# Moving four quads of V gathers per tile from the attention heads to the output and query projections, with the copy of the finished sums behind them

## The reference, cut to what matters

```python
q = (xb @ w_query).reshape(T, PEER_HEADS, 2, PEER_HALF)
s = jnp.einsum('thcd,hcnd->thcn', q, sub_keys)
sa, ia = lax.top_k(s[:, :, 0], PEER_TOPK)
...
top_s, top_j = lax.top_k(cand, PEER_TOPK)
eidx = jnp.take_along_axis(cidx, top_j, axis=-1)
gate = jax.nn.softmax(top_s.astype(jnp.float32), axis=-1).astype(xb.dtype)
act = jax.nn.gelu(jnp.einsum('thkd,td->thk', expert_u[eidx], xb), approximate=False)
return jnp.einsum('thk,thkd->td', gate * act, expert_v[eidx])
```

## Time and profile before

| what | value |
|---|---|
| median of 3 runs | 2177.47 us (2175.39 to 2177.49) |
| the profiled execution's own time | 2178.01 us |
| its span, first to last instruction | 2175.9 us |
| PE busy | 1216.6 us, 56% of the span |
| DVE busy | 1261.5 us, 58% |
| POOL busy | 1174.1 us, 54% |
| ACT busy | 374.3 us, 17% |
| moved by DMA | 722.04 MB, mean 332 GB/s |
| software DMA queue (the gathers) | 624.01 MB |

### The profile page before, as it was taken

How to read it: one execution, slowest core, us unless ns; L and a number is a source line. 1 busy time by engine, 2 the same in 40 slices (tenths; PEclk the granted TensorE clock), 3 DMA queues, 4 the chain that set the end, 5 groups by cost and what they waited for, 6 DMA issues and landing times.

```text
span 2175.9 us, 15704 instructions
## 1 busy us (share of the span) xinstructions
PE 1216.6 (56%) x4932; PEld 541.1 (25%) x4932; DVE 1261.5 (58%) x2795; ACT 374.3 (17%) x1034; POOL 1174.1 (54%) x1197
## 2 busy tenths in 40 slices
PE   5898778474885335853455574445667322223454
PEld 2544343233331233411222231122332000000110
DVE  3344430876485997776664678667477665555001
ACT  1221211011031011211121121112113100001211
POOL 3012110241457763577767457776745767777773
PEclk9798889785898557866567796666778656555887
DMA  9211274484899998999999999999999999999997
GB/s 338 94 59 39 77 275 133 164 302 162 343 372 379 410 380 321 371 361 410 409 389 403 410 384 371 410 409 395 408 411 349 375 409 409 409 409 409 411 409 295
DMA packets 204306, 722.04 MB, mean 332 GB/s; under 512 B 23248, under 2 KB 25536, under 8 KB 203072
## 3 DMA queue, kind: packets, MB, share of 16 engines
q0 software_dynamic: 171168, 624.01, 73.7%
q1 hardware_dynamic: 33056, 97.03, 12.1%
HBM read 704.71 MB, written 15.70 MB: 331 GB/s over the span
## 4 chain that ended last, share of the span: by engine, by line
PE 25%; DMA 24%; DVE 16%; POOL 14%; issue 5%; ACT 4%; DVEq 0%; POOLq 0%; ACTq 0%
DMA arena<-peer_expert_v,idx_v 16%; POOL arena L595 10%; DVE arena L1384 7%; PE PD L1041 6%; DMA arena<-peer_expert_u,idx_all 5%; POOL arena L589 4%; PE PB L1251 4%; PE PD L963 3%; PE PB L1230 3%; PE PA L1230 2%; DMA lev<-w_out 2%; PE PA L1181 2%; DMA lev<-peer_w_query 2%; DVE w L1521 1%; DVE lev L1501 1%
## 5 line engine op out<-in xcount | busy, mean ns | idle before, releaser
L589 POOL DMA_INDIRECT arena<-peer_expert_u,idx_all x576 | 545.5, 947 | 462.5 <-DVE arena L1384 218.7
L1384 DVE SCALAR_TENSOR_TENSOR arena<-arena,PC 128x1024 f32<-128x1024 f32 x576 | 675.5, 1217 | 149.7 <-DMA arena<-peer_expert_u,idx_all 143.8
L595 POOL DMA_INDIRECT arena<-peer_expert_v,idx_v x576 | 571.8, 993 | 252.0 <-issue 145.4
L1041 PE MATMUL PD<-arena,diag_v 128*32 128x512 f32 x1792 | 362.4, 887 | 516.5 <-DMA arena<-peer_expert_v,idx_v 490.7
L1041 PEld LDWEIGHTS PD<-arena,diag_v 128*32 128x32 f32 x1792 | 79.9, 141 | 758.8 <-issue 758.8
L817 ACT ACTIVATE diag_v<-consts,gate_all 128x32 f32<-128x32 f32 x576 | 138.1, 310 | 585.7 <-PE PD L1041 462.2
L963 PE MATMUL PD<-arena 128*128 128x512 f32 x384 | 175.8, 613 | 0.0
L1041 PE MATMUL PA<-arena,diag_v 128*32 128x512 f32 x512 | 87.0, 813 | 78.2 <-DMA arena<-peer_expert_v,idx_v 78.2
L1230 PE MATMUL PB<-lev,rows_t 128*128 128x512 f32 x160 | 86.6, 700 | 18.1 <-DMA lev<-w_out 12.4
L963 PEld LDWEIGHTS PD<-arena 128*128 128x128 f32 x384 | 74.0, 197 | 86.4 <-issue 85.9
L1449 DVE TENSOR_TENSOR PA<-PA,consts 128x128 f32<-128x128 f32 (+4 forms) x56 | 14.0, 250 | 139.1 <-PE PA L1099 138.8
(11 more groups left out here) (271 smaller groups left out, 1509.9 us busy)
## 6 DMA issues: line engine op xcount, KB each, us to landing
lev<-w_out SPq DMA_DIRECT2D x40, 512.0 KB, 9.2
lev<-peer_w_query SPq DMA_DIRECT2D x40, 512.0 KB, 7.8
arena<-w_in SPq DMA_DIRECT2D x8, 2048.0 KB, 14.2
arena<-peer_expert_u,idx_all POOLq DMA_INDIRECT x576, 9.7
arena<-peer_expert_v,idx_v POOLq DMA_INDIRECT x576, 10.2
arena<-w_in POOLq DMA_DIRECT2D x4, 2048.0 KB, 8.5
act<-staged SPq DMA_DIRECT2D x4, 1796.0 KB, 7.2
staged<-arena POOLq DMA_DIRECT2D x5, 1024.0 KB, 5.6
```

Source lines behind the costliest of these rows:

```text
L589: pool.indirect_dma_start(slot, None, peer_expert_u[0], bass.IndirectOffsetOnAxis(ap=idx_all[:, k:k + 1], axis=0)).then_inc(arrived, 16)
L595: pool.indirect_dma_start(slot, None, peer_expert_v[0], bass.IndirectOffsetOnAxis(ap=idx_v[:, k:k + 1], axis=0)).then_inc(arrived, 16)
L1041: ins = pe.matmul(psum[c * STRIP:(c + 1) * STRIP, half * 512:(half + 1) * 512], diag_v[:, at * STRIP:(at + 1) * STRIP], ring[slot_of[v_pla ...
L1384: eng.scalar_tensor_tensor(out=slot, in0=slot, scalar=1.0, in1=h2_dots[:, :], op0=ALU.mult, op1=ALU.mult, accum_out=out).then_inc(free, 1)
```

## The change

In tiles 3 and 4, four quads are taken from `head1`, `head3`, `head5` and `head7`. Two of them are placed at `rows`, between the output projection and the transposes of the normed rows, and two at `pq0`, between the halves of the query projection. The number of quads left over from `top` is 19 before and after. ACT's copy of the finished sums, which stood after `gram2`, now stands after `pq1`, behind the evacuation of the second query half. SP's store of them follows the last weight loads. ACT writes the diagonals of `pq0` ahead of its wait for the first query half. The copy and the store move in tiles 2, 3 and 4.

```diff
-LEFT_PLACES = [("start", 1)] + [(f"head{h}", 1) for h in range(HEADS)] + [
-    ("levels", 3), ("masks", 3), ("gram1", 2), ("gram2", 2)]
+LEFT_PLACES = [("start", 1)] + [(f"head{h}", 1) for h in range(0, HEADS, 2)] + [
+    ("levels", 3), ("masks", 3), ("gram1", 2), ("gram2", 2), ("rows", 2), ("pq0", 2)]
...
-            for place in [place for place, _ in DOT_PLACES + NEXT_PLACES] + ["end", "last", "rest"]:
+            for place in [place for place, _ in DOT_PLACES + [("pq0", 0)] + NEXT_PLACES] + ["end", "last", "rest"]:
...
-                if t > 1:
-
-                    sp.wait_ge(y_part_ready, t - 1)
-                    sp.dma_start(y_dram[t - 2], h2[:, :]).then_inc(y_part_saved, 16)
                 sp.wait_ge(x1_ready, t + 1)
                 sp.dma_start(x1_dram[t], xm).then_inc(x1_saved, 16)
...
                 for c in range(DC + WO_RING, 2 * DC):
                     sp.wait_ge(wo_used, 2 * DC * t + c - WO_RING + 1)
                     load_w_out(c)
+                if t > 1:
+
+                    sp.wait_ge(y_part_ready, t - 1)
+                    sp.dma_start(y_dram[t - 2], h2[:, :]).then_inc(y_part_saved, 16)
...
-                if t > 1:
-
-                    eng.wait_ge(v_free, values_before(t - 1))
-                    if t > 2:
-                        eng.wait_ge(y_part_saved, 16 * (t - 2))
-                    eng.activation(h2[:, :], PD[:, :], ACT.Copy).then_inc(y_part_ready, 1)
                 eng.wait_ge(ho_done, HG * (t + 1))
...
+                diagonals(t, "pq0")
                 eng.wait_ge(pq_done, t + 1)
                 nq = P if t else N_SAMPLE
                 eng.activation(w1[0:nq, 0:D], PB[0:nq, :], ACT.Copy).then_inc(pq_evac, 1)
-                diagonals(t, "pq0")
                 eng.wait_ge(wo_used, 2 * DC * (t + 1))
                 eng.activation(w1[0:nq, D:2 * D], PA[0:nq, :], ACT.Copy).then_inc(pq_evac, 1)
                 diagonals(t, "pq1")
+                if t > 1:
+
+                    eng.wait_ge(v_free, values_before(t - 1))
+                    if t > 2:
+                        eng.wait_ge(y_part_saved, 16 * (t - 2))
+                    eng.activation(h2[:, :], PD[:, :], ACT.Copy).then_inc(y_part_ready, 1)
```

## The result

The change makes the kernel slower: 2204.4 us median (2204.14 to 2206.64, 4 runs) against 2177.48 us (2175.39 to 2179.11, 4 runs). The ratio is 1.0124, 95% interval 1.0111 to 1.0138. That is 26.9 us more, where 2226 us was forecast with a range from 2206 to 2249. The direction was right and the place was right.

What follows compares the result with a forecast made beforehand. Gathers and loads at the memory limit (409 to 412 GB/s) bound heads and query stage. Per tile 36.2 + 4.4 + 0.8 = 41.4 us lost, 18 given back, 23.4 net; with tile 2's copy 47.6 us: 2226 us, range 2206 to 2249.

Steps and rivals of the forecast that it cites:

- The wait at the second quad: At `rows`, PE waits for gather number 32, so L1241 starts 36.2 us late in each of tiles 3 and 4.
- the count of ring places: At `rows`, POOL runs 17 gathers ahead: numbers 0 to 16 are in flight when it stops, number 32 comes later.
- The first quad: At `rows`, gathers 12 to 15 take 26.3 us, land at about 1250; multiplied in the shadow of the second quad.
- The rival in which the quads fit PE's gap: At `rows`, both quads fill PE's 6.61 us wait for DVE: about -14 us per tile, 2150 us; chance 4%.
- The quads between the halves: At `pq0`, rows have landed when PE comes and PE is warm: 4.4 us for two quads.
- The copy: On ACT ahead of L937, the moved copy delays PE's scores by 0.8 us in tiles 2, 3 and 4.
- The heads: Heads of tiles 3 and 4 lose 16 gathers each: 18 us given back per tile, ends 12 and 20.
- moving a gather gives nothing by itself: In stages at 409 GB/s, bytes stay the same, so only DMA idle time added or removed changes the time.
- Behind the scores nothing changes: `top` begins with 17 V rows in the ring before and after, so a delay is neither shortened nor lengthened there.
- The Trainium skill's figure: Landing of 512 KB in 3.2 us instead of 12.5: delay 9.3 us less per tile, 2207 us; not adopted.
- the first three: Low ends per tile: rows land as quickly as least loaded (-7.2), quad warm (-1.4), no wait for weights (-1.2 us).
- some 18 us shorter together: Sign expected in the profile after: heads of tiles 3 and 4 some 18 us shorter together.

Runs made afterwards that it cites:

- runs with one quad: Changed kernel, but only head7's quad moved per tile, to `rows`, its gathers behind the 25 U gathers: 2214.69 us, ratio 1.0163.
- the gathers first: Changed kernel with the gathers of the two quads at `rows` issued in front of the 25 U gathers, PE's order kept: 2182.29 us, ratio 1.0021.
- two-quad run: Changed kernel, but only the quads of head3 and head7 moved, both to `rows`, gathers ahead of the U gathers, diagonals early: 2153.04 us, ratio 0.9884.
- The pair with head7 and head0: Changed kernel, but one quad moved to `rows`, gathers ahead of the U gathers, diagonals early: head7's 2164.04 us, head0's 2169.35 us.

## Why the prediction was half right

- **The wait at the second quad: right.** Forecast was L1241 late by 36.2 us; it came 36.8 us later behind L1561 than before (38.1 less 1.3). Number 32 landed 34.6 us behind L1561, where 33.9 was forecast, so the count of ring places held: it is behind the reach of 17 buffers. The first quad landed later than forecast, 12.8 us behind L1561 instead of 7.3. It stayed in the shadow of the second, so the sum did not feel it, but PE's idling came as two waits of 18 us and not as one of 25. The runs with one quad (slower) and with the gathers first (5 us left of 27) show that the place in the list does it. The rival in which the quads fit PE's gap (4%) is answered by the two waits in the trace of the change.
- **The quads between the halves: right, and cheaper.** 3.57 us for both (1269.27 to L1230 at 1272.84) instead of 4.4.
- **L1251: not in the sum.** It took 14.00 us instead of 15.79, and the transposes ahead of it 1.46 instead of 1.97. Together that is 2.3 us in tile 3, against which stand 1.67 us of waiting for a weight block, about 1 us more than before. The granted clock was 1.00 of full over the product, that is 2.4 GHz, where from 1250 to 1262 before it was 0.97 and over the 6 us ahead of that 0.50, the level of 1.2 GHz. In the change PE had run the second quad and the transposes right before it, with no wait but the 1.1 us for ACT. In the two-quad run PE had run two quads at the full clock, but idled 3.04 us behind them and 1.11 us behind the transposes, and there the product took 16.31 us, from 1230 to 1234 at 0.50.
- **The copy: PE's scores wait 0.83 us for ACT, as forecast at 0.8.** Its own run was about 5 us slower than the kernel before, more than this explains, and that stays open.
- **The heads: the term that was mis-sized, and the step that failed.** The step was "16 gathers less per tile at 1.25 us each are 20.0 us at most", of which 18 was taken. Measured were 26.5 and 23.1 us, so 13.6 of the 19.0 us by which the spans miss the forecast (28.6 against 47.6) come from here. One part of the step was right: a head without a quad was to last 10.2 us from one L1449 to the next, and in tile 3 three of them last 10.1 us. Between the masks of `head0` and `head7` the stretch lost 15.8 and 16.4 us, for 12 gathers that are 15.0. The excess is behind the last head: from the mask of `head7` to L1561 it lost 10.9 and 7.0 us, for four gathers that are 5.0. The bound of 20 holds only for a POOL that never pauses in the stretch. My windows ended at 1125 and 1495, just ahead of the places where it does: at the end of the heads it waits for DVE's dots 5.1 and 3.6 us beyond its pace of 1.25 us, and in front of `out` 3.5 and 4.7 us. In the change these are 1.8, 2.1, 2.2 and 2.2 us, which makes 4.6 and 3.9 us less. With the 20.0 for the gathers that is 24.6 and 23.9 of the 26.5 and 23.1 measured. The run with the even heads' quads moved brings the pause back (4.0 and 7.9 us) and costs 10 us of the give-back. The pair with head7 and head0 points the same way with one quad. Over all kernels here the first pause is 3.6 to 9.0 us in the eight stretches that keep the quad of `head7`, and at most 3.2 us in the twenty that don't, so that this quad feeds it is shown. It is not the whole excess: tile 3 of the run with the even heads' quads moved gives back 23.3 us with the quad in place, and the pause in front of `out` goes its own way (5.3 us in tile 3 of the run with the gathers first). By which step the quad feeds the pause is only argued: DVE's mask of a head waits for scores that stand behind the previous quad, so DVE comes late to the dots whose buffers POOL needs. It fits that in tile 3 of the change the three masks behind a head without a quad wait for nothing, and the other five 3.3 to 8.3 us.
- **The rest of the miss** is in the query stages (4.7 us less than forecast, the items above) and in 1.6 us up to tile 2, with 0.8 us forecast there the other way, which is less than that stretch differs from kernel to kernel. The 1.7 us at the end go against it.
- **The sentence "moving a gather gives nothing by itself" was too short.** The hole at `top` was seen (240 GB/s), but the forecast did not ask what the hole is worth to a move that fits. The two-quad run says 17.8 us in two tiles. "Behind the scores nothing changes" left out the other sign of it: in the change the two `top` windows have 6.8 us more hole than before.
- **The Trainium skill's figure.** By the Trainium skill (DMA: Bandwidth & Descriptors, Anatomy of one DMA) the result would have been 2207 us, nearer to the measured one than mine. The trace doesn't agree with that figure under load: landing took 13.1 us here, not 3.2. It would have come near by luck, since its 18.6 us too little of waiting happen to stand against the 13.6 us that the heads' term lacked.
- **The range and the signs.** The low end of the sum was worked out as 2202 us, and the measured 2204.4 lies above that. The stated range began at 2206, since all low ends at once seemed unlikely; what came was none of the first three, but the heads' term beyond its end of 20. The sign of "some 18 us shorter together" for the heads of tiles 3 and 4 does not fit the prediction's own sum, which has 18 us in each tile.

## What to carry to other kernels

Before work is moved into an engine's gap, count on the issuer's list how many transfers stand between the last one already in flight and the one that the moved work needs. With a ring of 17 buffers number 32 landed 34.6 us behind L1561 here, whatever the engine's own gap is. To be among the 17 in flight is not enough either: numbers 12 to 15 landed 12.8 us behind it, since they were issued last before the stop and took 29.8 us, while numbers 0 to 7 were there in time. Where the work must go there, the order of the issues has to be moved with it, which here, with one ACT step, turned +27 us into -21 us. And when a stretch seems to run at the issuer's pace, look at its edges too: a bound of "n issues at this pace" leaves out the pauses in the stretch, which the moved work itself may be causing.

## What the runs showed of the hardware that was not expected

Gathers of 512 KB land in 12.5 to 15.2 us in a stage at 410 GB/s and in 26.3 us beside the weight streams, in the change even in 29.8 us, but in 5.3 us when the queue has run empty. I read it so that the time to landing is mostly the backlog. The matmuls of a quad take 3.64 us after 18 us of idling and 1.82 us (3.64 for two) in a busy stretch. So a wait on PE is paid a second time in the work right behind it, and the work after that can come out faster, as L1251 did in the change and did not in the two-quad run.
